# First weight block in halves, the second feed-forward's turn between products, and key-2 one-hots in pairs

## The chip, the cores and the metric

The kernel is one program on one NeuronCore of a Trainium2 chip. The metric is the device time of one execution in microseconds; the number that stands for a kernel is the median of its runs. All times below are microseconds from the start of the profiled execution's span unless they are marked otherwise.

## What is computed

Two blocks over 256 tokens of width 1024, all in float32:

```
h = x
f = swiglu(rmsnorm(h), ffn1_w_gu, ffn1_w_down)        # 1024 -> 2 x 2816 -> 1024
h = h + 0.5 * rmsnorm(f)
m = hybrid_mixer(rmsnorm(h))                          # attention and state space
h = h + rmsnorm(m)
c = memory_cross_attention(rmsnorm(h), rmsnorm(mem))
h = h + rmsnorm(c)
f = swiglu(rmsnorm(h), ffn2_w_gu, ffn2_w_down)        # the second feed-forward
h = h + 0.5 * rmsnorm(f)
# second block
x = x + mix @ w_out                                   # short convolution and HGRN2
x = x + peer_ffn(rmsnorm(x), wq, keys, u, v)          # product keys, 128 x 128 experts
return rmsnorm(x)
```

In `peer_ffn` each token picks 16 x 8 pairs (key 1, key 2) with gates. The expert weight of a token is gelu(h u) times its gate, and the result is the sum over all 16,384 experts of weight times v. The kernel computes all experts densely and multiplies by a gate matrix (128 keys 1 by 128 keys 2) for each token.

## The kernel before, in words

**Weights.** All large matrices are one stream of 532 blocks of 128 x 1024 f32 (512 KB). SP loads them into a ring of four slots (lines 368 to 384). Each product in float32 is made of three products in the fast f32r form, so each block is split first: ScalarE copies it to `w_high` (L503, helper `split`), VectorE subtracts to get `w_low` (L1049, the same helper on VectorE). `product` (L1848 to L1850) then makes three matmuls: high x high, high x low, low x high. Semaphores count: `w_high`, `w_split` (low part done; SP waits for it before it loads the slot again) and `w_used` (PE done with a block; ScalarE waits for it before it splits into the slot again).

**Activations.** Rows are tokens in two tiles of 128. Before a feed-forward the tile is transposed on PE, eight 128 x 128 transposes into PSUM (`turn_tile`, L1869). ScalarE copies each one with its gain to `xT_high` (`highs`, L540), VectorE makes `xT_low` (`lows`, L1088). PE waits for the low parts it needs (`turned`).

**Order.** Each engine has its own program, an order written out by hand, and waits on semaphores only; what stands behind a waiting instruction waits too. The order around the change is:

- Start. SP issues: left half of tile 0's rows, the small column table `cols` (gains), ring block 0, right half of tile 0's rows, block 1, tile 1's rows, blocks 2 and 3, and more. PE: `turn_tile(0, 0)` (all eight transposes, the last four wait for the right half), then `ffn_up` with `panel_by_tile`: for tile 0 the blocks 0 to 3 (two k tiles each, six matmuls of 512 columns a block), with `turn_tile(0, 1)` after block 0; then the same four blocks for tile 1. ScalarE: high copies of k tiles 0 to 3, split of block 0, high copies 4 to 7, splits 1 to 3, high copies of tile 1, two squares of the rows, then the splits of panel 1 (lines 609 to 624). VectorE the same with the low parts (lines 1163 to 1175).
- Second feed-forward. The output product of the cross attention ends with `rows_tail`: the last four blocks for tile 0, then for tile 1 (24 matmuls). VectorE adds tile 0's result to `h` (`post_add`, L1135, L1141, L1143), splits blocks 0 and 1 of the new panel, makes tile 0's low parts, splits block 2, adds tile 1's result, splits block 3, makes tile 1's low parts (lines 1435 to 1444). ScalarE: split 0 to 2, high copies of tile 0, square of tile 1's result, split 3, high copies of tile 1, two squares of `h`, then the splits of panel 1 (lines 815 to 825). PE: `turn_tile(6, 0)` after the tail, the products of blocks 0 to 2 for tile 0, `turn_tile(6, 1)`, block 3, then tile 1.
- Gated steps. From u block 66 on, PE alternates one u block (24 matmuls of 256 columns) with `gates`: for a group of four tokens eight f16 matmuls of 128 columns (L2459, L2460) that place the gates of one token at (key 2, key 1). The stationary operand is `one_at_key2` (OB), a one-hot of key 2 for each token; the moving one is the gate at key 1, in a high (OAH) and a low f16 part (OAL). VectorE makes the key-1 one-hot (`hot1`, L1730), the key-2 one-hot (`hot2`, L1738), the low gates (L1747), multiplies gates into the weights (L1756, L1767) and splits one weight block (L1049) a step. ScalarE makes gelu (L957), a weight copy and four gate copies (L967). The key-1 one-hots and OAL lie with two tokens innermost; the key-2 one-hots lie token by token. After the last u block PE waits for the last groups' operands and begins the v blocks (`v_half`); VectorE's last `hot2` there stands before the first low part of the expert weights (L1803).

The longest single names: `h_done` counts VectorE's result updates, `xt_ps` groups of four transposes, `xt_high` and `xt_low` single k tiles.

Of the kernel before, what the change touches and what calls it, by code (L numbers as in the profile page):

```python
# [16 lines left out]
P = 128  # L17
# [58 lines left out]
TAIL = 4  # L76
EPS_COL = 60
# [29 lines left out]
def build(nc, stream, w_dt, cols, small_row, rows, x, mem, keys, out):  # L107
# [127 lines left out]
    OB = sb("one_at_key2", [P, 2, GROUP, P], 68.5, F16)  # L235
# [47 lines left out]

    def hidden_psum(p):

        o = 1024 + (p - 9) * 512 if p >= FFN_PANELS - 2 else 2048 + p % 2 * 512
        return PS[:, o:o + 512]
# [21 lines left out]
    loaded = [sem(f"loaded{i}") for i in range(SLOTS)]  # L310
    w_high, w_split, w_used = sem("w_high_done"), sem("w_split_done"), sem("w_used")
# [7 lines left out]
    eps_ok, rms_ok, xn_ok, factor_ok = sem("eps_ok"), sem("rms_ok"), sem("xn_ok"), sem("row_factor_ok")  # L319
    xt_ps, xt_high, xt_low = sem("xT_psum"), sem("xT_high_done"), sem("xT_low_done")  # L320
# [46 lines left out]
    def _(sp):  # L367
        sp.dma_start(H[:, 0, 0:512], x[0:P, 0:512]).then_inc(x_in, 16)
        sp.dma_start(COLS[:], cols).then_inc(const_in, 16)
        sp.dma_start(RING[:, 0, :], stream[0]).then_inc(loaded[0], 16)  # L370
# [122 lines left out]
    def _(act):  # L493
# [41 lines left out]
        def highs(k, gain, tt, high=XTH, kts=range(KT)):  # L535

            for kt in kts:
                if kt % 4 == 0:
                    act.wait_ge(xt_ps, 4 * k + 2 * tt + kt // 4 + 1)
                act.activation(high[:, kt, tt * P:(tt + 1) * P], xt_psum(k, tt)[:, kt, :], ACT.Copy,  # L540
# [67 lines left out]

        act.preload_act_table_set("sqrt_and_others")
# [3 lines left out]
        split(0, 1)  # L613
# [428 lines left out]
    def _(dve):  # L1042
# [39 lines left out]
        def lows(k, gain, tt, high=XTH, low=XTL, kts=range(KT)):  # L1082

            t = slice(tt * P, (tt + 1) * P)
            for kt in kts:
                if kt % 4 == 0:
                    dve.wait_ge(xt_high, 16 * k + 8 * tt + kt + 4)
                dve.scalar_tensor_tensor(low[:, kt, t], xt_psum(k, tt)[:, kt, :],  # L1088
# [48 lines left out]
        def post_add(k, tt, factor, acc=ACC):  # L1137
# [4 lines left out]
                                           ROWG[:], ALU.mult, ALU.mult))  # L1142
            dve.scalar_tensor_tensor(H[:, tt, :], TMP[:, tt, :], factor, H[:, tt, :],  # L1143
# [22 lines left out]
        split(0, 1)  # L1166
# [271 lines left out]
        split(b + 4, 2)  # L1438
        lows(6, "ffn2", 0)
# [293 lines left out]
        def hot2(g, dyn=None):  # L1733

            if dyn is not None or g >= 2:
                dve.wait_ge(g_ps, at(g - 1, dyn))
            t = bass.ds(at(GROUP * g, dyn, GROUP), GROUP)
            dve.tensor_tensor(OB[:, g % 2, :, :], IOTA[:].unsqueeze(1).to_broadcast([P, GROUP, P]),  # L1738
                              KEY_T[:, 1, t].unsqueeze(2).to_broadcast([P, GROUP, P]),
                              ALU.is_equal).then_inc(key2_ok, 1)  # L1740
# [104 lines left out]
    def _(pe):  # L1845
# [6 lines left out]
        def turn_tile(k, tt, kts=range(KT)):  # L1852
# [3 lines left out]
            elif k == 6:  # L1856
                pe.wait_ge(h_done, 5 + tt)
# [8 lines left out]
            for kt in kts:  # L1866
                if k == 0 and tt == 0 and kt == 4:
                    pe.wait_ge(x_right_in, 16)
                last = pe.transpose(xt_psum(k, tt)[:, kt, :], rows[:, tt, kt * P:(kt + 1) * P], IDENT[:])  # L1869
                if kt % 4 == 3:  # L1870
# [711 lines left out]
```

## Time and profile before

| | |
|---|---|
| median of 3 runs | 1685.05 us (1684.35 to 1688.13) |
| the profiled execution, its own time | 1690.22 us |
| its span | 1688.2 us |
| PE busy | 1659.6 us, 98% |
| PE weight loads busy | 1477.2 us, 88% |
| VectorE busy | 1183.8 us, 70% |
| ScalarE busy | 935.7 us, 55% |
| GpSimd busy | 49.5 us, 3% |
| DMA | 286.78 MB, 170 GB/s over the span |

Busy times of PE overlap, since matmuls are pipelined and their ends are modelled. The distance from one start to the next tells more than the duration of one. A timeline row gives the start, the duration (of a group of equal instructions, all of it), engine, line, operation, output <- inputs, and in brackets how long the engine had been idle and what released it. In rows of groups the last numbers are busy us, mean ns of one, and idle us before them.

### The profile page before, as it was taken

What the parts mean: (1) busy time and instruction counts of PE and PEld (TensorE: products, weight loads), DVE (VectorE), ACT (ScalarE), POOL (GpSimd) and SP (SyncE); (2) the same over time, 40 slices, a digit from 0 to 9 for tenths busy, and PEclk for the clock granted to TensorE, in tenths of its full rate; (3) what the DMA queues carried; (4) which work ended last, traced back from release to release, by engine and by line L of the source; (5) the groups of instructions that cost most, each with busy time, mean ns of one, the idle gap of its engine ahead of it and who ended that gap; (6) DMA issues with size and microseconds to landing.
All of it is one profiled execution on the core that took longest, in us unless ns stands there. A gap on an engine that the chain in (4) does not pass through costs nothing.

```text
span 1688.2 us, 30628 instructions
## 1 busy us (share of the span) xinstructions
PE 1659.6 (98%) x10348; PEld 1477.2 (88%) x10348; DVE 1183.8 (70%) x1920; ACT 935.7 (55%) x1566; POOL 49.5 (3%) x44
## 2 busy tenths in 40 slices
PE   8999999999999999989999999999999999999998
PEld 6888898898898788879989999999999888888887
DVE  5555686598565655466665799989999866666664
ACT  6445545476655644456364444467777655555554
POOL 0000003000000000010010000100000000000000
PEclk9999999999999999999999999999999999999999
DMA  7555463333453555545354445454444465555553
GB/s 271 188 182 185 172 203 112 113 103 135 150 200 114 199 187 185 188 145 185 118 175 163 168 166 201 162 172 152 161 149 159 150 200 192 193 193 192 194 191 125
DMA packets 79101, 286.78 MB, mean 170 GB/s; under 512 B 8896, under 2 KB 9152, under 8 KB 78912
## 3 DMA queue, kind: packets, MB, share of 16 engines
q1 hardware_dynamic: 78176, 282.27, 49.1%
q0 software_dynamic: 864, 3.67, 0.6%
q8 instruction: 41, 0.67, 0.2%
q14 instruction: 20, 0.16, 0.0%
HBM read 284.86 MB, written 1.05 MB: 169 GB/s over the span
## 4 chain that ended last, share of the span: by engine, by line
PE 93%; DVE 4%; ACT 2%; issue 1%; DMA 0%; POOL 0%; SPq 0%; ACTq 0%; DVEq 0%; POOLq 0%
PE ps L1848 29%; PE ps L1850 28%; PE ps L1849 28%; DVE w_low L1049 1%; PE ps L2459 1%; PE ps L2460 1%; PE ps L1869 1%; PE ps L1951 1%; ACT w_high L503 1%; PE ps L2424 0%; PE ps L2231 0%; PE ps L2093 0%; PE ps L2111 0%; PE ps L2250 0%; DVE tmp L1141 0%
## 5 line engine op out<-in xcount | busy, mean ns | idle before, releaser
L1049 DVE TENSOR_TENSOR w_low<-ring,w_high 128x1024 fp32r<-128x1024 f32 x532 | 653.2, 1232 | 314.3 <-ACT w_high L503 312.4
L503 ACT ACTIVATE w_high<-ring 128x1024 fp32r<-128x1024 f32 x532 | 558.7, 1055 | 297.2 <-PE ps L1850 285.7
L1848 PE MATMUL ps<-xT_high,w_high 128*128 128x256 f32 x1472 | 424.1, 288 | 0.0
L1849 PE MATMUL ps<-xT_high,w_low 128*128 128x256 f32 x1472 | 416.8, 283 | 0.0
L1850 PE MATMUL ps<-xT_low,w_high 128*128 128x256 f32 x1472 | 416.6, 283 | 0.0
L1848 PEld LDWEIGHTS ps<-xT_high,w_high 128*128 128x128 f32 x1472 | 282.4, 192 | 2.0 <-issue 1.6
L1849 PEld LDWEIGHTS ps<-xT_high,w_low 128*128 128x128 f32 x1472 | 282.6, 192 | 0.7 <-issue 0.5
L1850 PEld LDWEIGHTS ps<-xT_low,w_high 128*128 128x128 f32 x1472 | 282.5, 192 | 0.0
L1848 PE MATMUL ps<-w_high,expert_w_high 128*128 128x512 f32 x512 | 199.9, 391 | 0.2 <-DVE expert_w_low L1803 0.2
L1850 PE MATMUL ps<-w_low,expert_w_high 128*128 128x512 f32 x512 | 199.7, 390 | 0.0
L1849 PE MATMUL ps<-w_high,expert_w_low 128*128 128x512 f32 x512 | 199.7, 390 | 0.0
L1848 PE MATMUL ps<-w_high,xT_high 128*128 128x512 f32 x464 | 186.5, 402 | 5.2 <-DVE xT_low L1088 4.2
L1850 PE MATMUL ps<-w_low,xT_high 128*128 128x512 f32 x464 | 183.0, 394 | 0.0
L1849 PE MATMUL ps<-w_high,xT_low 128*128 128x512 f32 x464 | 182.8, 394 | 0.0
L1017 ACT ACTIVATE expert_w_high<-expert_w 128x256 fp32r x124 | 51.8, 418 | 164.9 <-PE ps L1850 164.9
L1848 PEld LDWEIGHTS ps<-w_high,expert_w_high 128*128 128x128 f32 x512 | 96.5, 188 | 20.4 <-issue 0.5
L1849 PEld LDWEIGHTS ps<-w_high,expert_w_low 128*128 128x128 f32 x512 | 96.4, 188 | 20.2
L1850 PEld LDWEIGHTS ps<-w_low,expert_w_high 128*128 128x128 f32 x512 | 96.4, 188 | 20.0
L1821 DVE TENSOR_TENSOR expert_w_low<-expert_w,expert_w_high 128x256 fp32r<-128x256 f32 x124 | 52.7, 425 | 82.2 <-ACT expert_w_high L1017 82.2
L1848 PEld LDWEIGHTS ps<-w_high,xT_high 128*128 128x128 f32 x464 | 88.6, 191 | 24.7 <-issue 4.6
L1850 PEld LDWEIGHTS ps<-w_low,xT_high 128*128 128x128 f32 x464 | 88.4, 190 | 19.2
L1849 PEld LDWEIGHTS ps<-w_high,xT_low 128*128 128x128 f32 x464 | 88.6, 191 | 17.4
(404 smaller groups left out, 2227.5 us busy)
## 6 DMA issues: line engine op xcount, KB each, us to landing
ring<-in_stream SPq DMA_DIRECT2D x532, 512.0 KB, 3.4
row_gain<-in_rows POOLq DMA_DIRECT2D x4, 512.0 KB, 4.5
mem_sb<-in_mem SPq DMA_DIRECT2D x1, 1024.0 KB, 9.8
keys_sb<-in_keys POOLq DMA_DIRECT2D x1, 1024.0 KB, 5.2
h<-in_x SPq DMA_DIRECT2D x2, 256.0 KB, 3.9
h<-in_x SPq DMA_DIRECT2D x1, 512.0 KB, 6.9
last_gain<-in_rows POOLq DMA_DIRECT2D x1, 512.0 KB, 4.3
out<-result SPq DMA_DIRECT2D x1, 512.0 KB, 2.6
```

The source lines that it names most:

```text
L503: act.activation(WH[:, n % SLOTS, :], RING[:, n % SLOTS, :], ACT.Copy).then_inc(w_high, 1)
L1017: act.activation(WTH[:, v % 4, :], slot, ACT.Copy).then_inc(wt_high, 1)
L1049: dve.tensor_tensor(WL[:, n % SLOTS, :], RING[:, n % SLOTS, :], WH[:, n % SLOTS, :].bitcast(F32), ALU.subtract).then_inc(w_split, 1)
L1821: dve.tensor_tensor(WTL[:, v % 4, :], slot, WTH[:, v % 4, :].bitcast(F32), ALU.subtract).then_inc(wt_low, 1)
L1848: pe.matmul(out, high, w_hi, start=start, stop=False, skip_group_check=True)
L1849: pe.matmul(out, low, w_hi, start=False, stop=False, skip_group_check=True)
L1850: return pe.matmul(out, high, w_lo, start=False, stop=stop, skip_group_check=True)
L1869: last = pe.transpose(xt_psum(k, tt)[:, kt, :], rows[:, tt, kt * P:(kt + 1) * P], IDENT[:])
L1951: last = pe.transpose(hidden_psum(p)[:, o:o + P], HN[:, parity, tt, ft * P:(ft + 1) * P], IDENT[:])
L2459: pe.matmul(PS[:, o:o + P], OB[:, g % 2, j, :], OAH[:, g % 2, j, :], start=True, stop=False)
L2460: last = pe.matmul(PS[:, o:o + P], OB[:, g % 2, j, :], OAL[:, g % 2, j // 2, :, j % 2], start=False, stop=True)
```

## The change

What it does, part by part:

- **Start.** The load of `cols` is issued by ScalarE ahead of its table load. Block 0 is loaded in two halves of 512 columns, both ahead of the right half of tile 0's rows; ScalarE and VectorE split each half by itself. Tile 0's k tiles 0 to 3 are transposed into pairs of their own PSUM banks and copied pair by pair. Tile 0's k tiles 4 to 7 are transposed after block 0's products, tile 1's after block 1's.
- **Second feed-forward.** The result update of that stage is made in two halves with a semaphore each. `turn_tile(6, 0)` is moved ahead of the last block of the output product's tail, in two halves, into pairs of banks. VectorE splits one block, makes four low parts, splits one block, makes the other four. Tile 1's transposes are made four after block 2 and four after block 3.
- **Gated steps.** `one_at_key2` gets the layout of the key-1 one-hots, [pair, key, 2 tokens], and is compared against the f16 iota; PE reads it at a step of two values.

```diff
+HALVED = (2,)
...
-    OB = sb("one_at_key2", [P, 2, GROUP, P], 68.5, F16)
+    OB = sb("one_at_key2", [P, 2, GROUP // 2, P, 2], 68.5, F16)
...
+    def by_pairs(k, tt):
+        return k in (0, 6) and tt == 0
+    def xt_tile(k, tt, kt):
+        if by_pairs(k, tt):
+            o = 1024 + kt // 2 * 512 + kt % 2 * P
+            return PS[:, o:o + P]
+        return xt_psum(k, tt)[:, kt, :]
...
         sp.dma_start(H[:, 0, 0:512], x[0:P, 0:512]).then_inc(x_in, 16)
-        sp.dma_start(COLS[:], cols).then_inc(const_in, 16)
-        sp.dma_start(RING[:, 0, :], stream[0]).then_inc(loaded[0], 16)
+        sp.dma_start(RING[:, 0, 0:512], stream[0][:, 0:512]).then_inc(first_in, 16)
+        sp.dma_start(RING[:, 0, 512:1024], stream[0][:, 512:1024]).then_inc(loaded[0], 16)
         sp.dma_start(H[:, 0, 512:1024], x[0:P, 512:1024]).then_inc(x_right_in, 16)
...
             for kt in kts:
-                if kt % 4 == 0:
+                if by_pairs(k, tt) and kt < 4:
+                    if kt % 2 == 0:
+                        act.wait_ge(xt_pair, k // 3 + kt // 2 + 1)
+                elif kt % 4 == 0:
                     act.wait_ge(xt_ps, 4 * k + 2 * tt + kt // 4 + 1)
...
+        act.dma_start(COLS[:], cols).then_inc(const_in, 16)
         act.preload_act_table_set("sqrt_and_others")
         act.wait_ge(eps_ok, 1)
         act.wait_ge(const_in, 16)
         highs(0, "ffn1", 0, kts=range(0, 4))
-        split(0, 1)
+        act.wait_ge(first_in, 16)
+        act.activation(WH[:, 0, 0:512], RING[:, 0, 0:512], ACT.Copy).then_inc(first_high, 1)
+        act.wait_ge(loaded[0], 16)
+        act.activation(WH[:, 0, 512:1024], RING[:, 0, 512:1024], ACT.Copy).then_inc(w_high, 1)
         highs(0, "ffn1", 0, kts=range(4, 8))
         split(1, 3)
...
             for kt in kts:
-                if kt % 4 == 0:
+                if by_pairs(k, tt):
+                    if kt % 2 == 0:
+                        dve.wait_ge(xt_high, 16 * k + 8 * tt + kt + 2)
+                elif kt % 4 == 0:
                     dve.wait_ge(xt_high, 16 * k + 8 * tt + kt + 4)
...
+            if k in HALVED:
+                for half, done in enumerate((h_left, h_done)):
+                    w = slice(half * 512, half * 512 + 512)
+                    dve.scalar_tensor_tensor(H[:, tt, w], TMP[:, tt, w], factor, H[:, tt, w],
+                                             ALU.mult, ALU.add).then_inc(done, 1)
+                return
...
         lows(0, "ffn1", 0, kts=range(0, 4))
-        split(0, 1)
+        for half, high, low in ((0, first_high, first_low), (1, w_high, w_split)):
+            w = slice(half * 512, half * 512 + 512)
+            dve.wait_ge(high, 1)
+            dve.tensor_tensor(WL[:, 0, w], RING[:, 0, w], WH[:, 0, w].bitcast(F32), ALU.subtract).then_inc(low, 1)
...
         post_add(2, 0, 1.0)
-        split(b + 4, 2)
-        lows(6, "ffn2", 0)
+        split(b + 4, 1)
+        lows(6, "ffn2", 0, kts=range(0, 4))
+        split(b + 5, 1)
+        lows(6, "ffn2", 0, kts=range(4, 8))
         split(b + 6, 1)
...
-            t = bass.ds(at(GROUP * g, dyn, GROUP), GROUP)
-            dve.tensor_tensor(OB[:, g % 2, :, :], IOTA[:].unsqueeze(1).to_broadcast([P, GROUP, P]),
-                              KEY_T[:, 1, t].unsqueeze(2).to_broadcast([P, GROUP, P]),
-                              ALU.is_equal).then_inc(key2_ok, 1)
+            dve.tensor_tensor(OB[:, g % 2, :, :, :], IOTA16[:].unsqueeze(1).to_broadcast([P, GROUP // 2, P, 2]),
+                              pairs(KEY_T[:, 1, :], g, dyn), ALU.is_equal).then_inc(key2_ok, 1)
...
             elif k == 6:
-                pe.wait_ge(h_done, 5 + tt)
+                if 0 in kts:
+                    pe.wait_ge(h_left, tt + 1)
+                if 4 in kts:
+                    pe.wait_ge(h_done, 5 + tt)
...
                     for kt in (2 * n, 2 * n + 1):
+                        if tt == 0 and b + n == 0:
+                            pe.wait_ge((first_low, w_split)[kt], 1)
...
                     if tt:
                         last.then_inc(w_used, 1)
+                    elif norm == 0 and n == 0:
+                        turn_tile(0, 0, range(4, 8))
+                    elif norm == 6 and n == turn_after:
+                        turn_tile(norm, 1, range(0, 4))
+                    elif norm == 6 and n == turn_after + 1:
+                        turn_tile(norm, 1, range(4, 8))
                     elif n == turn_after:
                         turn_tile(norm, 1)
...
             last.then_inc(acc0_done, 1)
             for kt in range(kts - TAIL, kts):
+                if turn is not None and kt == kts - 1:
+                    turn_tile(turn, 0, range(0, 4))
+                    turn_tile(turn, 0, range(4, 8))
                 row_block(stage, kt, 1, high, low, acc, kts).then_inc(w_used, 1)
...
-        turn_tile(0, 0)
-        ffn_up("ffn1_up", 0, 0, 0)
+        turn_tile(0, 0, range(0, 4))
+        ffn_up("ffn1_up", 0, 0, 1)
...
-        rows_tail("xa_o", 8)
-        turn_tile(6, 0)
+        rows_tail("xa_o", 8, turn=6)
...
-                pe.matmul(PS[:, o:o + P], OB[:, g % 2, j, :], OAH[:, g % 2, j, :], start=True, stop=False)
-                last = pe.matmul(PS[:, o:o + P], OB[:, g % 2, j, :], OAL[:, g % 2, j // 2, :, j % 2],
+                pe.matmul(PS[:, o:o + P], OB[:, g % 2, j // 2, :, j % 2], OAH[:, g % 2, j, :], start=True, stop=False)
+                last = pe.matmul(PS[:, o:o + P], OB[:, g % 2, j // 2, :, j % 2], OAL[:, g % 2, j // 2, :, j % 2],
                                  start=False, stop=True)
```

## Rows read from the trace of the kernel before

**Rows 1.** The page, part 1: busy us, share, instructions.
```profile
PE 1659.6 (98%) x10348; PEld 1477.2 (88%) x10348; DVE 1183.8 (70%) x1920; ACT 935.7 (55%) x1566; POOL 49.5 (3%) x44
```
**Rows 2.** Waits of PE: waiter <- releaser, us in total, times, longest.
```profile
PE ps L1848 <- DVE xT_low L1088: 4.2, 2, 2.6
```
**Rows 3.** The chain that ended last, at the start: start us, us, what.
```profile
1.74 4.98 DMA ring<-in_stream
```
**Rows 4.** Timeline of PE at the start.
```profile
3.59 1.09 PE L1869 MATMUL ps<-ident,h 128*128 128x128 f32 x4 [3.59 <-DMA h<-in_x]
...
9.11 0.80 PE L1848 MATMUL ps<-w_high,xT_high 128*128 128x512 f32 x1 [0.52 <-DVE w_low L1049]
...
11.84 1.91 PE L1869 MATMUL ps<-ident,h 128*128 128x128 f32 x8
13.40 0.78 PE L1848 MATMUL ps<-w_high,xT_high 128*128 128x512 f32 x1
...
14.74 0.40 PE L1848 MATMUL ps<-w_high,xT_high 128*128 128x512 f32 x1
...
18.15 0.39 PE L1848 MATMUL ps<-w_high,xT_high 128*128 128x512 f32 x1
```
**Rows 5.** Timeline of ScalarE at the start.
```profile
4.80 1.14 ACT L540 ACTIVATE xT_high<-ps,cols 128x128 fp32r<-128x128 f32 x4 [2.71 <-PE ps L1869]
...
8.62 1.15 ACT L540 ACTIVATE xT_high<-ps,cols 128x128 fp32r<-128x128 f32 x4 [0.82 <-PE ps L1869]
9.64 1.07 ACT L503 ACTIVATE w_high<-ring 128x1024 fp32r<-128x1024 f32 x1
```
**Rows 6.** Timeline of VectorE at the start.
```profile
10.85 1.21 DVE L1049 TENSOR_TENSOR w_low<-ring,w_high 128x1024 fp32r<-128x1024 f32 x1
```
**Rows 7.** Groups of ScalarE, shapes apart: busy us, mean ns | idle.
```profile
L659 ACT ACTIVATE xn<-ssd_out 128x512 f32<-128x512 f32 x4 | 2.5, 629 | 0.1
```
**Rows 8.** Groups of VectorE, shapes apart.
```profile
L1738 DVE TENSOR_TENSOR one_at_key<-iota,keysT 128x512 f16<-128x512 f32 x64 | 43.4, 679 | 0.0
...
L1730 DVE TENSOR_TENSOR one_at_key<-iota,keysT 128x512 f16<-128x512 f16 x64 | 26.6, 416 | 0.9 <-ACT gate_low L991 0.9
```
**Rows 9.** Timeline of VectorE at the second feed-forward.
```profile
544.48 2.35 DVE L1049 TENSOR_TENSOR w_low<-ring,w_high 128x1024 fp32r<-128x1024 f32 x2
...
553.20 1.22 DVE L1049 TENSOR_TENSOR w_low<-ring,w_high 128x1024 fp32r<-128x1024 f32 x1
...
559.92 2.36 DVE L1049 TENSOR_TENSOR w_low<-ring,w_high 128x1024 fp32r<-128x1024 f32 x2 [0.79 <-ACT w_high L503]
```
**Rows 10.** Timeline of ScalarE at the second feed-forward.
```profile
554.02 2.18 ACT L540 ACTIVATE xT_high<-ps,cols 128x128 fp32r<-128x128 f32 x8 [3.41 <-PE ps L1869]
...
558.84 3.92 ACT L503 ACTIVATE w_high<-ring 128x1024 fp32r<-128x1024 f32 x4
```
**Rows 11.** Timeline of PE at the second feed-forward.
```profile
554.46 0.50 PE L1848 MATMUL ps<-w_high,xT_high 128*128 128x512 f32 x1
...
561.44 0.39 PE L1848 MATMUL ps<-w_high,xT_high 128*128 128x512 f32 x1
```
**Rows 12.** Timeline of PE in one gated step.
```profile
1203.63 0.28 PE L1850 MATMUL ps<-xT_low,w_high 128*128 128x256 f32 x1
1203.75 0.23 PE L2459 MATMUL ps<-gate_high_at_key,one_at_key 128*128 128x128 f16 x1
...
1204.19 0.36 PE L1848 MATMUL ps<-xT_high,w_high 128*128 128x256 f32 x1
```
**Rows 13.** Busy time by stretch: us; PE, PEld, DVE, ACT, POOL; clock, DMA.
```profile
1180.00:1230.00 50.00, 50.00 (x475) 49.36 (x474) 49.82 (x90) 37.33 (x90) 0.00 (x0) 1.00 0.44 153
```
**Rows 14.** Timeline of PE after the last u block.
```profile
1331.80 0.23 PE L2459 MATMUL ps<-gate_high_at_key,one_at_key 128*128 128x128 f16 x1 [2.11 <-ACT gate_high_at_key L967]
...
1332.79 0.76 PE L1848 MATMUL ps<-w_high,expert_w_high 128*128 128x512 f32 x1 [0.24 <-DVE expert_w_low L1803]
```
**Rows 15.** Busy time by stretch, there; the clock is the third number from the end.
```profile
1335.00:1336.00 1.00, 1.00 (x5) 0.76 (x4) 0.83 (x3) 0.00 (x0) 0.00 (x0) 0.71 0.01 4
```

More of the change, by code:

```diff
@@ L310, in build @@
     loaded = [sem(f"loaded{i}") for i in range(SLOTS)]
+    first_in, first_high, first_low = sem("first_half_loaded"), sem("first_half_high"), sem("first_half_split")
     w_high, w_split, w_used = sem("w_high_done"), sem("w_split_done"), sem("w_used")
@@ L319, in build @@
     eps_ok, rms_ok, xn_ok, factor_ok = sem("eps_ok"), sem("rms_ok"), sem("xn_ok"), sem("row_factor_ok")
+    xt_pair, h_left = sem("xT_psum_first_pairs"), sem("h_left_done")
     xt_ps, xt_high, xt_low = sem("xT_psum"), sem("xT_high_done"), sem("xT_low_done")
@@ L537, in highs @@
             for kt in kts:
-                if kt % 4 == 0:
+                if by_pairs(k, tt) and kt < 4:
+                    if kt % 2 == 0:
+                        act.wait_ge(xt_pair, k // 3 + kt // 2 + 1)
+                elif kt % 4 == 0:
                     act.wait_ge(xt_ps, 4 * k + 2 * tt + kt // 4 + 1)
-                act.activation(high[:, kt, tt * P:(tt + 1) * P], xt_psum(k, tt)[:, kt, :], ACT.Copy,
+                act.activation(high[:, kt, tt * P:(tt + 1) * P], xt_tile(k, tt, kt), ACT.Copy,
                                scale=COLS[:, GAIN_COL[gain] + kt:GAIN_COL[gain] + kt + 1]).then_inc(xt_high, 1)
@@ L1085, in lows @@
             for kt in kts:
-                if kt % 4 == 0:
+                if by_pairs(k, tt):
+                    if kt % 2 == 0:
+                        dve.wait_ge(xt_high, 16 * k + 8 * tt + kt + 2)
+                elif kt % 4 == 0:
                     dve.wait_ge(xt_high, 16 * k + 8 * tt + kt + 4)
-                dve.scalar_tensor_tensor(low[:, kt, t], xt_psum(k, tt)[:, kt, :],
+                dve.scalar_tensor_tensor(low[:, kt, t], xt_tile(k, tt, kt),
                                          COLS[:, GAIN_COL[gain] + kt:GAIN_COL[gain] + kt + 1],
@@ L1868, in turn_tile @@
                     pe.wait_ge(x_right_in, 16)
-                last = pe.transpose(xt_psum(k, tt)[:, kt, :], rows[:, tt, kt * P:(kt + 1) * P], IDENT[:])
-                if kt % 4 == 3:
-                    last.then_inc(xt_ps, 1)
+                last = pe.transpose(xt_tile(k, tt, kt), rows[:, tt, kt * P:(kt + 1) * P], IDENT[:])
+                if by_pairs(k, tt) and kt in (1, 3):
+                    last.then_inc(xt_pair, 1)
+                elif kt % 4 == 3:
+                    last.then_inc(xt_ps, 2 if by_pairs(k, tt) else 1)
         def turned(k, tt, kts):
@@ L1921, in panel_by_tile @@
                     s = (b + n) % SLOTS
-                    if tt == 0:
+                    if tt == 0 and b + n:
                         pe.wait_ge(w_split, b + n + 1)
@@ L1988, in rows_product, with rows_tail @@
                 row_block(stage, kt, 1, high, low, acc, kts).then_inc(w_used, 1)
-        def rows_tail(stage, kts, high=HTH, low=HTL, acc=ACC, halves=None):
+        def rows_tail(stage, kts, high=HTH, low=HTL, acc=ACC, halves=None, turn=None):
             for kt in range(kts - TAIL, kts):
```

## The prediction

> **What bounds the kernel now.** I read the page first. TensorE is busy for 98% of the span [rows 1], and the chain that ended last runs almost wholly over PE, so what counts is where PE stands still. PE's waits by releaser come next: apart from the first input rows, the largest is 4.2 us for VectorE's low parts of the turned activations, in two places [rows 2]. The change touches three places, read in their timelines: the start, the entry to the second feed-forward at 544 to 562 us, and the gated steps at 1121 to 1337 us.
>
> At the start the chain is: the first weight block lands at 6.72 [rows 3], ScalarE copies it, VectorE subtracts, PE starts its first product at 9.11 [rows 4]. All eight transposes of tile 0 are done by then. The six products of block 0 are followed by the eight transposes of tile 1, and block 1 starts at 13.40, tile 1 at 18.15 [rows 4]. The spacing of products tells the clock: six take 11.84 - 9.11 = 2.73 us, 0.43 each, which for 512 columns is 1.2 GHz; from 14.74 they stand 0.227 apart ((18.15 - 14.74) / 15), which is 2.4 GHz (the recorded granted clock reads 1.0 throughout this stretch, so the spacing is the witness). So the lower level costs 0.47 us per us.
>
> **Part A, the start.** Moving the small column table to ScalarE's queue costs one issue there (about 0.4 us before its table load) and ScalarE has nothing to do until 4.80 [rows 5]: nothing. On SP's queue one issue leaves and one comes, so every later load is issued as before; the split block moves in shorter rows, and block 1's copy stands at 9.64 with later copies waiting for loads; I expect them under 0.5 us later, and they will be needed 2 us later (below): nothing.
>
> 1. Four transposes take 1.09 us from 3.59 [rows 4], about 0.21 apart, so the first pair ends at 4.25, not 4.68. The high copies start 0.12 later, at 4.37, and take 1.02 us to the next instruction (8.62 to 9.64) [rows 5]: the left half's copy starts at 5.39 if the half has landed. That load is shown nowhere: it lies between the first rows' landing (3.59) and the whole block's (6.72) [rows 3, 4]; as it is half the bytes, issued 0.47 earlier, I take 4.9, in time.
> 2. A copy of 512 columns takes 0.63 [rows 7], a subtraction of that width 0.68 [rows 8]: copy to 6.02, low parts of two pairs to about 6.2, subtraction to 6.9, first product at 6.95. That is 2.15 earlier than 9.11. The right half follows in time even if it lands at 6.72.
> 3. But tile 0's right transposes now stand **behind** the six products of block 0, and ScalarE's program has their high copies ahead of block 1's copy. So: products to 6.95 + 2.73 = 9.7; four transposes 1.1, to 10.8; high copies 1.02, block 1's copy from 11.8 to 12.9 (1.07 [rows 5]); its subtraction 1.21 [rows 6], to 14.15. Block 1 starts at 14.2: **0.8 later** than 13.40. And tile 1's eight transposes, done before 13.40 in the old order, still lie ahead: 0.87 at the full clock (half of the 1.56 from 11.84 to 13.40, with its start-up).
> 4. PE is idle from 10.8 to 14.2. Before, PE worked on from 9.11 and the clock rose 5.4 us later (the row at 14.74 is the first short one). Elsewhere, PE resumes at 1331.80 after 2.11 us of idleness, is recorded below full clock, and is back during 1335 to 1336 (0.71, so at about 1335.4), 3.6 us later [rows 14, 15]. I take 4.5 us between these. From 14.2, 18 products and 8 transposes need 18 x 0.227 + 0.87 = 4.95 us at full clock, plus 0.47 x 4.5 = 2.1: tile 1 starts at 21.25, **3.1 us later** than 18.15.
>
> Bounds of A: full clock at once gives 19.15, +1.0; a left half that lands only at 6.72 (+1.2) with the lag of 5.4 gives +4.7. Behind it ScalarE's squares end at about 23.0, and its first copy of panel 1, needed with its subtraction by 26.7, is ready by 25.3: hidden.
>
> **Part B, the second feed-forward.** The old order waits here for low parts before its first product, the shorter of the two waits (4.2 - 2.6 = 1.6 us [rows 2]). The new one transposes tile 0 ahead of the last block of the output product and so starts about 1.4 earlier, near 546.6. But VectorE then sets the pace. Its work from 544.48 to 553.20 [rows 9] is the same: three subtractions, eight low parts, one result update. Its one idle stretch, waiting for the high copies, shrinks only by what the split updates cost more, as ScalarE is busy with a weight copy until then. So block 3's subtraction still starts at 553.2 and block 3's products at 554.4, as before (554.46 [rows 11]): the early start turns into waits of 0.35, 0.85, 0.7 and 1.3 us.
>
> What is new comes behind. Four of tile 1's transposes moved from VectorE's shadow to after block 3: tile 1 starts at 554.4 + 1.5 + 0.45 = 556.4. Their high copies, until now made at 554.02 to 556.04 [rows 10], end at 556.7 + 1.0 = 557.7. Then come two squares, 2.80 us to the first copy of panel 1 (556.04 to 558.84 [rows 10]): 560.5 instead of 558.84. Its subtraction came out at 559.92 + 1.23 = 561.15 [rows 9] for a PE that began panel 1 at 561.44 [rows 11], which is 0.25 of slack. Now it comes out 1.66 later, at 562.8. PE would have wanted it at 561.85, so panel 1 starts at about 562.85: **+1.4 us**. Bounds: +0.4 (the transposes alone) and +2.9 (PE works 0.45 of the 2.5 us before 554.4, and should the clock fall there, block 3 and the transposes take 1.5 longer).
>
> **Part C, key-2 one-hots.** The operation goes from f32 compare to the packed form of the key-1 one-hots: 679 to 416 ns [rows 8], 0.26 us a step. In the loop VectorE shows 49.82 of 50 us busy but PE 50.00 [rows 13], with no wait, so it buys nothing there. Only at the end does it lie on the chain: PE waits 0.24 for the first low part of the weighted experts, right after such a one-hot [rows 14]: **-0.2 us**. TensorE now loads those one-hots at a step of two values. The rows show no such load; bounds are nothing and the rival below. I take nothing, since the moving operand of every second product is already read at that step and the eight products take 0.44 us [rows 12], evenly spaced.
>
> **The sum**: 3.1 + 1.4 - 0.2 = **+4.3 us**. The profiled execution took 1690.22 us (span 1688.2), 5.2 above the median of 1685.05; the difference carries over: 1689.4.
>
> **Rivals.**
> - Clock back early (0.18). PE works 3.8 us before its pause at the start, more than the 3.6 us of the other place. For: that figure. Against: the idle stretch after it is longer than the 2.11 us that cost the clock before. A is then +1.0, the sum +2.2: 1687.3.
> - More lost (0.15): late left half, slow clock at both places, about +6.5: 1691.6.
> - VectorE holds the gated loop (0.08), the one that ends on the other side, not slower. Place: 61 steps. PE's own work in a step is 24 products 0.12 apart and eight in 0.44 [rows 12], 3.32; a step takes about 3.37 (475 starts in 50 us at 32 a step [rows 13]). If these 0.05 to 0.07 are waits that the trace doesn't mark, a VectorE 0.26 faster gives them all back, -3 to -4.3; it decides if VectorE's step is the longer by any amount. With A and B it ends within 1.5 us of before: 1686. Against: PE shows no idle time and the first product after the one-hots is 0.08 longer wherever it stands.
> - Slow weight loads (0.08). If spaced f16 weights load as f32 ones do, whose products stand 0.12 apart [rows 12], eight take 0.96 instead of 0.44: 64 x 0.52 = +33, 1722. No row here decides between the two; by the first reading the sum would be that of this rival, by the second it stays.
> - The start pays off as drawn up, through an order that I misread (0.06): -2.2 and less, 1682.
>
> **Chances.** About 0.2% (3.4 us) is what a measurement of this kernel can tell from no change. My forecast has 0.45, mostly (0.36) beyond 3.4 us; with "more lost" and slow loads: slower 0.60. Same: the rest of the forecast, the early clock and the held loop: 0.33. Faster: 0.07. The range leaves out slow loads and the last rival: 1685.0 to 1694.0, A's and B's bounds included for the most part.
>
> **What would show it.** Start: first product near 7.0; a PE idle stretch of over 3 us before block 1, released by w_low after xT_high copies; block 1 near 14.2; products 0.43 apart until about 18.7; tile 1 near 21. Second feed-forward: first product near 546.6, then waits for w_low and h; block 3 unmoved against the start of the stage; panel 1 1.4 later with a wait for w_low behind ScalarE's squares. Gates: L1738's successor at about 416 ns, step length and product spacing unchanged, VectorE with 0.26 us of idle time a step. I am wrong if block 1 starts before 13.4, if the second feed-forward's first up panel ends earlier than before, or if the step changes.

## The result and the profile after

| | before | after |
|---|---|---|
| median of 11 runs each | 1687.41 us | 1692.12 us |
| lowest to highest | 1684.02 to 1691.1 | 1690.95 to 1693.0 |
| the profiled execution, its own time (span) | 1690.22 (1688.2) | 1693.0 (1691.0) |

The ratio is 1.0025, with a 95% interval of 1.0016 to 1.0034: slower by about 4.2 us (2.7 to 5.7 by the interval; the medians differ by 4.7), forecast +4.3. In this comparison the kernel before itself came out at 1687.41, 2.4 above the median of three runs that the forecast started from, so the absolute number is 2.7 above the forecast of 1689.4 and inside its range.

The page after: the engines' busy time, and, from the view of waits, four groups of PE's waits (us in total, times, longest).

```profile
PE 1659.6 (98%) x10348; PEld 1476.1 (87%) x10348; DVE 1170.5 (69%) x1923; ACT 934.3 (55%) x1567; POOL 49.4 (3%) x44
```

```profile
PE ps L1881 <- DVE w_low L1070: 6.6, 6, 3.4
PE ps L1905 <- DMA h<-in_x: 4.0, 1, 4.0
...
PE ps L1881 <- DVE xT_low L1112: 2.6, 1, 2.6
PE ps L1881 <- DVE w_low L1199: 2.3, 1, 2.3
```

Two more groups of that view, of the kernel before:

```profile
PE ps L1869 <- DMA h<-in_x: 6.4, 2, 3.6
...
PE ps L1848 <- DVE w_low L1049: 1.8, 4, 0.7
```

PE is busy as long as before; VectorE is busy 13 us less. PE waits 2.4 us less for input rows and 1.6 less for low parts of the activations (4.2 in [rows 2], 2.6 after), but for low parts of **weights** 6.6 + 2.3 = 8.9 us instead of 1.8. The balance is 3.1 more.

**The start.** The timeline of PE after, from the first transposes to tile 1 (21.19), and the granted clock (third number from the end) in two windows of it:

```profile
4.03 1.09 PE L1905 MATMUL ps<-ident,h 128*128 128x128 f32 x4 [4.03 <-DMA h<-in_x]
7.42 0.77 PE L1881 MATMUL ps<-w_high,xT_high 128*128 128x512 f32 x1 [2.30 <-DVE w_low L1199]
...
10.11 1.02 PE L1905 MATMUL ps<-ident,h 128*128 128x128 f32 x4
14.56 0.79 PE L1881 MATMUL ps<-w_high,xT_high 128*128 128x512 f32 x1 [3.43 <-DVE w_low L1070]
...
17.29 1.28 PE L1905 MATMUL ps<-ident,h 128*128 128x128 f32 x8
18.33 0.48 PE L1881 MATMUL ps<-w_high,xT_high 128*128 128x512 f32 x1
18.65 0.40 PE L1882 MATMUL ps<-w_high,xT_low 128*128 128x512 f32 x1
...
21.19 0.39 PE L1881 MATMUL ps<-w_high,xT_high 128*128 128x512 f32 x1
```

```profile
14.00:15.00 1.00, 0.43 (x1) 0.44 (x2) 1.00 (x2) 1.00 (x2) 0.00 (x0) 0.69 1.06 383
...
17.00:18.00 1.00, 1.00 (x7) 0.80 (x6) 0.00 (x0) 0.00 (x0) 0.00 (x0) 0.61 0.73 213
```

The first product starts 1.69 earlier than before, block 1 starts 1.16 later, tile 1 3.04 later (9.11, 13.40, 18.15 in [rows 4]). ScalarE and VectorE in the same stretch:

```profile
11.17 1.14 ACT L557 ACTIVATE xT_high<-ps,cols 128x128 fp32r<-128x128 f32 x4 [4.09 <-PE ps L1905]
12.18 2.96 ACT L517 ACTIVATE w_high<-ring 128x1024 fp32r<-128x1024 f32 x3
```

```profile
13.28 3.50 DVE L1070 TENSOR_TENSOR w_low<-ring,w_high 128x1024 fp32r<-128x1024 f32 x3 [0.33 <-ACT w_high L517]
```

ScalarE is idle for 4.09 us for want of the right transposes, with block 1's copy queued behind them. Only at 12.18 does that copy begin, and PE has its low part at 14.56. The granted clock falls at about 14.4, after PE has stood still for three microseconds, and is back at about 17.8, 3.2 us after block 1 began.

**The second feed-forward.** PE's rows with waits, and ScalarE's (block 3 begins at 557.39, the four transposes behind it at 558.89):

```profile
553.53 0.50 PE L1881 MATMUL ps<-w_high,xT_high 128*128 128x512 f32 x1 [0.49 <-DVE w_low L1070]
555.65 0.66 PE L1905 MATMUL ps<-ident,h 128*128 128x128 f32 x4 [0.46 <-DVE h L1170]
557.39 0.50 PE L1881 MATMUL ps<-w_high,xT_high 128*128 128x512 f32 x1 [1.08 <-DVE w_low L1070]
...
565.75 0.47 PE L1881 MATMUL ps<-w_high,xT_high 128*128 128x512 f32 x1 [0.80 <-DVE w_low L1070]
```

```profile
559.53 1.14 ACT L557 ACTIVATE xT_high<-ps,cols 128x128 fp32r<-128x128 f32 x4 [2.04 <-PE ps L1905]
...
563.31 3.89 ACT L517 ACTIVATE w_high<-ring 128x1024 fp32r<-128x1024 f32 x4
```

The stage comes 3.03 late (the x32 group at 520.03 instead of 517.00). With that taken off, panel 1 (565.75) starts 1.28 later than the 561.44 of [rows 11], after a wait of 0.80 behind ScalarE's squares. To compare stretches, I use the time from the x32 group ahead of the cross attention's output to the first group of turns of the feed-forward's hidden values. The chain that ended last has these rows before:

```profile
517.00 6.91 PE ps L2250 x32
...
572.49 0.44 PE ps L1951 x4
```

and these after, so the stretch grew from 55.49 to 56.85:

```profile
520.03 6.91 PE ps L2299 x32
...
576.88 0.44 PE ps L1997 x4
```

**The gated steps.** The groups of VectorE from 1140 to 1320 us, the key-2 one-hots, and the window that answers to [rows 13]:

```profile
L1772 DVE TENSOR_TENSOR one_at_key<-iota,keysT 128x512 f16<-128x512 f16 x53 | 21.9, 413 | 0.0
```

```profile
1180.00:1230.00 50.00, 50.00 (x471) 49.35 (x470) 46.78 (x89) 36.68 (x89) 0.00 (x0) 1.00 0.45 157
```

679 became 413 ns, and VectorE's busy time in 50 us fell from 49.82 to 46.78, while PE is as full as it was.

### The profile page after: what moved, and what is told of

Its sections match the earlier page's. It is cut to its first block, busy times and chain, and to the rows that moved or that the text cites. A ratio compares the mean times of both kernels' runs of the same rounds, so it can differ in the third digit from the quotient of the medians.

```text
span 1691.0 us, 30634 instructions
## 1 busy us (share of the span) xinstructions
PE 1659.6 (98%) x10348; PEld 1476.1 (87%) x10348; DVE 1170.5 (69%) x1923; ACT 934.3 (55%) x1567; POOL 49.4 (3%) x44
## 3 DMA queue, kind: packets, MB, share of 16 engines
q0 software_dynamic: 864, 3.67, 0.7%
## 4 chain that ended last, share of the span: by engine, by line
PE 93%; DVE 4%; ACT 2%; issue 1%; DMA 0%; POOL 0%; ACTq 0%; DVEq 0%; POOLq 0%
PE ps L1881 28%; PE ps L1882 28%; PE ps L1883 28%; DVE w_low L1070 1%; PE ps L2507 1%; PE ps L2508 1%; PE ps L1905 1%; ACT w_high L517 1%; PE ps L1997 1%; PE ps L2472 0%; PE ps L2280 0%; PE ps L2142 0%; PE ps L2160 0%; PE ps L2299 0%; DVE tmp L1165 0%
```

## The experiments

All kernels ran on one core, beside runs of the kernel before. What the texts on record call "the changed kernel" is the kernel after. Product, copy and turn lines shift by a few from kernel to kernel.

**1. Each part alone.** The start alone, then the second feed-forward alone, then the one-hots alone; the diff of the change is cut to that part.

> The start's part of the change alone. If the new order of the start costs what the changed kernel shows there (my theory): block 1's first product at 14.2 to 14.6, products 0.43 apart until about 18, tile 1 at 21.2 (18.15 before), every later stage up to the second feed-forward 3.0 us late, and the second feed-forward no further behind; ratio to before 1.0018. Rival, chance clock dips make the difference of the two kernels: ratio within 0.1% of 1.

Median 1693.39, ratio 1.0034 (1.0022 to 1.0046), above the 1.0018 that I expected and above the whole change. Block 1 at 14.76, tile 1 at 21.82: +3.67. The second feed-forward's stretch is 55.53, as before. The nine times lie in two groups, 1690.65 to 1691.87 with a mean granted clock of 0.995 or 0.996 (four runs) and 1693.39 to 1694.13 with 0.992 or 0.993 (five), and the median falls into the second. Why five of nine lie there isn't shown.

> The second feed-forward's part alone. My theory: block 3's products start where they did (554.4), tile 1 of panel 0 at 556.2, panel 1 at 562.8 instead of 561.4 with a PE wait of about 0.8 us for w_low behind ScalarE's two squares; +1.4 us from there on, ratio 1.0008. Rival, the early start of block 0 is kept: panel 1 at 560 to 561.

Median 1689.44, ratio 1.0008 (0.9997 to 1.0019). The stretch is 56.87: +1.38.

> The key-2 one-hots in pairs alone. My theory: L1738's operation at 413 ns, loads of these one-hots at 96 to 97 ns as before, gated step unchanged at 3.39 us, PE's wait before the first expert product 0.25 shorter: -0.2 us in all, ratio 0.9999. Rival, VectorE held the loop: step at 3.32 to 3.34, ratio 0.998.

Median 1686.78, ratio 0.9998 (0.9989 to 1.0008). One-hots 414 ns. The last gate's product to the first product of the experts fell from 0.56 (1332.23 to 1332.79 before) to 0.31, the forecast -0.25.

So by the traces each part does alone what it does in the sum. The ratios alone wouldn't show this: they add up to 1.0040 where the whole change has 1.0025, and those of the last two can't be told from 1.

**2. Block 1's parts ahead of the right rows' parts.** The kernel after with, on both ScalarE and VectorE:

```
+        split(1, 1)
         highs(0, "ffn1", 0, kts=range(4, 8))
-        split(1, 3)
+        split(2, 2)
```

> The changed kernel with one swap at the start: ScalarE's copy of block 1 and VectorE's subtraction stand ahead of the high and low parts of tile 0's right k tiles. My theory: block 1's copy starts when its load lands (about 9.0), its subtraction ends at 11.3, block 1's products at 11.4 instead of 14.56, the clock up near 12.8, tile 1 at 17.2 (21.19 in the changed kernel, 18.15 before): 4 us less than the changed kernel, ratio to before 1.0002. Rival, loads in shorter rows or the column table's other queue are the cost: block 1 no earlier than 13.

Median 1689.59, ratio 1.0003 (0.9992 to 1.0014). PE's timeline:

```profile
7.89 0.77 PE L1883 MATMUL ps<-w_high,xT_high 128*128 128x512 f32 x1 [2.30 <-DVE w_low L1200]
...
11.22 0.47 PE L1883 MATMUL ps<-w_high,xT_high 128*128 128x512 f32 x1
11.54 0.39 PE L1884 MATMUL ps<-w_high,xT_low 128*128 128x512 f32 x1
...
14.90 0.50 PE L1883 MATMUL ps<-w_high,xT_high 128*128 128x512 f32 x1 [1.18 <-DVE w_low L1071]
...
17.80 0.39 PE L1883 MATMUL ps<-w_high,xT_high 128*128 128x512 f32 x1
```

Block 1 follows with no wait, 3.3 us earlier, the products stand 0.23 apart from there on, and tile 1 starts 3.4 earlier. Tile 1 is 0.6 later than I expected, as block 2 now waits 1.18 behind the high copies. That the queue order behind the moved transposes makes the start's loss is shown by this: same halves, same moved transposes, same queue for the column table, no loss.

**3. The clock's share of it.** The kernel after with eight products behind the right transposes whose result is never read:

```
+                        for _ in range(8):
+                            pe.matmul(PS[:, 3072:3584], XTH[:, 0, 0:P], WH[:, 0, 0:512], start=True, stop=True)
```

> The changed kernel with eight products of 512 columns more, behind tile 0's right transposes at the start; their result is never read, they only keep TensorE busy while it otherwise waits for block 1. If the share of the start's loss that I put down to the clock is right (from 14.56 to 21.19 us the products and transposes take 6.6 us where full clock needs 4.95), block 1 starts at 14.5 to 14.9 as in the changed kernel, its products stand 0.23 us apart at once, and tile 1 starts at 19.4 to 20.0 instead of 21.2: ratio about 1.0016. If the clock has no part in it, tile 1 stays at 21.2 or later and the ratio at 1.0025.

Median 1689.89, ratio 1.0021 (1.0011 to 1.0031). PE:

```profile
11.05 2.08 PE L1974 MATMUL ps<-w_high,xT_high 128*128 128x512 f32 x8
14.73 0.50 PE L1881 MATMUL ps<-w_high,xT_high 128*128 128x512 f32 x1 [1.61 <-DVE w_low L1070]
15.07 0.39 PE L1882 MATMUL ps<-w_high,xT_low 128*128 128x512 f32 x1
...
19.86 0.39 PE L1881 MATMUL ps<-w_high,xT_high 128*128 128x512 f32 x1
```

Block 1 comes when it did (14.73 beside 14.56), since the eight products unblock nothing. But the products stand 0.23 apart at once, and tile 1 starts at 19.86 instead of 21.19. With block 1's 0.17 taken off, the clock lost in the pause is 1.5 of the 3.04, and the rest is the pause itself. The granted clock of the kernel after agrees: it lost 1.7 us between 14 and 18 us, and nothing is recorded there here. I forecast 2.1 for the clock. The median, 1.0021, can't be told from the 1.0025 of the kernel after; this rests on the traces.

**4. Tile 1 turned in one piece after block 2.** The kernel after with:

```
                     elif norm == 6 and n == turn_after:
-                        turn_tile(norm, 1, range(0, 4))
-                    elif norm == 6 and n == turn_after + 1:
-                        turn_tile(norm, 1, range(4, 8))
+                        turn_tile(norm, 1)
```

> The changed kernel with one thing undone in the second feed-forward: tile 1's eight transposes all stand after weight block 2, none after block 3. My theory of the loss there (four transposes behind block 3, so ScalarE's high copies of tile 1, its two squares and its copy of panel 1 all start later, and TensorE waits for panel 1's low part) expects the stretch from the first x32 group of the cross attention (520.03 in the changed kernel) to the group of turns behind the feed-forward (576.88) to shrink from 56.85 to 55.5 to 55.9 us, as it was before (55.49), and no wait for w_low at panel 1. The rival, that the loss comes from turning tile 0 early (split updates, a pause of TensorE that costs it its clock), expects 56.5 to 57. Ratio to the kernel before: 1.0017 by the theory, 1.0025 by the rival.

The timeline of PE and of ScalarE:

```profile
556.67 1.06 PE L1905 MATMUL ps<-ident,h 128*128 128x128 f32 x8 [1.15 <-DVE h L1170]
557.72 0.51 PE L1881 MATMUL ps<-w_high,xT_high 128*128 128x512 f32 x1
```

```profile
562.15 1.99 ACT L517 ACTIVATE w_high<-ring 128x1024 fp32r<-128x1024 f32 x2
```

The stage begins at 520.36 here (0.33 later than in the kernel after) and yet panel 1's copies begin at 562.15 instead of 563.31. PE shows no wait behind the turn, and the stretch is 55.45: the loss is gone, though tile 0 is still turned early and `h` still updated in halves. The theory holds in the trace. The time doesn't show the gain: median 1691.7, ratio 1.0033 (1.0023 to 1.0043), where I had expected 1.0017. Its profile lost 1.7 us more to the clock elsewhere than that of the kernel after (experiment 7), and of its other nine runs three have a mean granted clock as low (0.992 or 0.993). The other six have 0.996 and average 1691.3 us; the six runs of the kernel after at 0.996 average 1691.8. So at an equal clock 0.5 of the 1.4 us shows in the times, and where the rest stays is open.

**5. A kernel with the gains and without the losses.** The kernel before with the split first block and the start's moved transposes, experiment 2's order and the paired one-hots.

> The kernel before with the split first block, block 1's copy and subtraction ahead of those of tile 0's right rows, and the key-2 one-hots two tokens innermost; the second feed-forward as before. If the two losses are where I put them (block 1 queued behind the right rows; tile 1's transposes behind block 3), this keeps the gains and has neither loss: block 1 at 11.2 to 11.8, tile 1 at 17.2 to 17.9 (18.15 before), the feed-forward's stretch 55.5, the last gate step 0.25 shorter: 0.5 to 1.2 us faster than before, ratio 0.9993 to 0.9997. If a shared cause that I have not found is at work, it stays above 1.0005.

Block 1 at 11.17, tile 1 at 17.63, the stretch 55.55. Median 1688.39, ratio 1.0008 (0.9999 to 1.0017): not faster, against my 0.9993 to 0.9997. I had compared its start with the 18.15 of one profile; the five profiles with the old start (experiment 7) have tile 1 at 17.74 on average, so its start gains 0.1, and part C (-0.25 at the end, +0.4 from the spaced loads of experiment 6) costs it that. The clock adds to that: its twelve runs have a mean granted clock of 0.9951, the 33 runs of before beside them 0.9958. That is 1.2 us, about what the ratio shows. Then the same with work for PE ahead of its first product:

```
+        for _ in range(5):
+            pe.matmul(PS[:, 3072:3200], IDENT[:], IDENT[:], start=True, stop=True)
         turn_tile(0, 0, range(0, 4))
+        for _ in range(5):
+            pe.matmul(PS[:, 3072:3200], IDENT[:], IDENT[:], start=True, stop=True)
```

> The previous kernel with five transposed identity products of 128 columns ahead of the first four transposes and five behind them; their result is never read, they only give TensorE work before its first product. If the clock at the start comes up by how long TensorE has been at work, the six first products stand 0.23 us apart rather than 0.43 in part or whole, and tile 1 starts 0.5 to 1.3 us earlier than in the previous kernel (if block 1's data is there; else block 1 waits for it and gains less than 0.5). If it comes up at a fixed lag after the first product only, nothing changes: tile 1 at 17.2 to 17.9.

PE's timeline:

```profile
1.60 2.50 PE L2056 MATMUL ps<-ident 128*128 128x128 f32 x10 [1.60 <-POOL ident L416]
...
7.98 0.59 PE L1881 MATMUL ps<-w_high,xT_high 128*128 128x512 f32 x1 [0.17 <-DVE w_low L1200]
8.41 0.40 PE L1882 MATMUL ps<-w_high,xT_low 128*128 128x512 f32 x1
...
11.53 0.50 PE L1881 MATMUL ps<-w_high,xT_high 128*128 128x512 f32 x1 [1.36 <-DVE w_low L1071]
```

The first products stand 0.23 apart instead of 0.43: the clock follows what PE did before them. Up to block 1 all of that is given back, as block 1 now isn't ready (a wait of 1.36): from the first product to block 1 it takes 3.55 us, and 3.62 without the early work. What stays is block 1's own products at the full clock and fewer later waits. Tile 1 starts at 16.95, 0.68 earlier, and the median is 1686.7, ratio 1.0 (0.9991 to 1.0009): level with before.

**6. The spaced weight load.** Comparing long stretches of steps showed something that single rows hide. Sixty gated steps in the kernel before and in the one with the pairs alone:

```profile
1125.86 0.23 PE L2459 MATMUL ps<-gate_high_at_key,one_at_key 128*128 128x128 f16 x1 [0.95 <-ACT gate_high_at_key L967]
...
1329.06 0.23 PE L2459 MATMUL ps<-gate_high_at_key,one_at_key 128*128 128x128 f16 x1
```

```profile
1119.55 0.23 PE L2457 MATMUL ps<-gate_high_at_key,one_at_key 128*128 128x128 f16 x1 [0.94 <-ACT gate_high_at_key L967]
...
1323.14 0.23 PE L2457 MATMUL ps<-gate_high_at_key,one_at_key 128*128 128x128 f16 x1
```

203.20 / 60 = 3.387 us, and 203.59 / 60 = 3.393. All kernels with pairs have the second, all without the first. One kernel keeps VectorE's slow f32 compare but writes to the spaced layout, which PE reads as in the change:

```
-            dve.tensor_tensor(OB[:, g % 2, :, :], IOTA[:].unsqueeze(1).to_broadcast([P, GROUP, P]),
+            dve.tensor_tensor(OB[:, g % 2, :, :, :].rearrange("p a k b -> p a b k"), IOTA[:].unsqueeze(1).unsqueeze(1).to_broadcast([P, GROUP // 2, 2, P]),
```

> The kernel before with its key-2 one-hots written at a step of two values (so TensorE loads them spaced, as in the changed kernel), but from the f32 table and by the f32 compare, so that VectorE's operation stays slow. A gated step takes 3.387 us in every kernel without the pairs and 3.393 in every one with them. If the spaced load is the cause, the step here is 3.393; if VectorE's shorter operation is (its traffic or its timing beside TensorE), it stays at 3.387. Either way the last gate step to the first expert product is 0.55 us as before, or more.

One run, 1688.69 us. The groups of VectorE and PE's weight loads from 1140 to 1320, and the window of 50 us:

```profile
L1738 DVE TENSOR_TENSOR one_at_key<-iota,keysT 128x512 f16<-128x512 f32 x54 | 41.3, 766 | 0.0
```

```profile
L2459 PEld LDWEIGHTS ps<-gate_high_at_key,one_at_key 128*128 128x128 f16 x212 | 19.4, 97 | 2.3
```

```profile
1180.00:1230.00 50.00, 50.00 (x475) 49.36 (x474) 50.00 (x89) 36.72 (x89) 0.00 (x0) 1.00 0.46 157
```

Sixty steps run from 1123.60 to 1327.20: 3.393. So the spaced operand costs 6.6 ns a step, some 0.4 us in all, whatever VectorE does. And VectorE, with its one-hots at 766 ns and busy for 50.00 of 50, still doesn't lengthen the step: it doesn't hold the loop.

**7. The two kernels once more, and the account.** The times scatter by 7 us within a kernel, and experiments 4 and 5 came out above their traces.

> The kernel before, profiled once more. The three kernels so far that keep its start show tile 1 at 18.15, 18.52 and 16.98 us, and the ten profiles so far lose their clock in pieces of 1.7 us. If the start's scatter is that of the first rows' landing and of the moment at which the clock rises, tile 1 starts between 16.9 and 18.6 again, the second feed-forward's stretch is 55.5 us and a gated step 3.387 us to within 0.002. With the lost clock taken off, the span is 1678.0 plus the difference of tile 1 to 18.15, within 0.3. If the scatter lies elsewhere, that sum misses by more.

> The changed kernel, profiled once more. By the accounts (start, second feed-forward, gated steps, lost clock in pieces of 1.7 us) tile 1 starts between 21.0 and 21.9 us, the second feed-forward's stretch is 56.85, a gated step 3.393, and with the lost clock taken off the span is 1682.5 plus the difference of tile 1 to 21.19, within 0.3. If the changed kernel's loss were chance of its first profile, one of these misses.

A window of the first profile of before (the last three numbers are PE's clock, the DMA share and GB/s), and PE's rows around it:

```profile
250.00:251.00 1.00, 1.00 (x7) 1.00 (x7) 1.00 (x4) 0.89 (x2) 0.00 (x0) 0.57 0.05 16
```

```profile
247.56 0.17 PE L1848 MATMUL ps<-w_dt_high,xT_high 128*128 128x16 f32 x1
...
250.41 0.36 PE L1849 MATMUL ps<-w_dt_high,xT_low 128*128 128x16 f32 x1
...
255.31 0.77 PE L1848 MATMUL ps<-w_high,xT_high 128*128 128x512 f32 x1
```

PE shows as busy without a gap, and its granted clock falls to 0.50 for some ten us. But what keeps it busy from 247.56 to 255.31 are 48 products of only 16 columns (the state space's step sizes, `w_dt`), 0.11 us apart at first and 0.21 at half clock; it falls 2.6 us into them. All 13 profiles have the 48 products and the fall there. In seven the fall comes 2.3 to 2.8 us after the first of them and the clock stays down for about 10.2 us; in four it comes after 3.3 to 4.4 us and lasts 6.8; in the two others (before again, pairs alone) after 5.1 to 5.2 us, at their end, and lasts 3.4.

I summed (1 - granted clock) over every window of 2 us between 50 and 1680 us. In all 13 profiles the loss comes in pieces of 1.7 us: one to three around 250 us; one or two near 742, where PE is idle for 1.5 and 2.6 us around eight transposes; one near 802 in three kernels, at the end of 32 products of 32 rows; one near 1331 in all but one, after 2.1 us of idleness. (The start, before 50 us, is left out, as tile 1's row accounts for it.) With these taken off, the spans fit a sum of 1678.0 (the first profile of before: 1688.2 - 10.2) + (tile 1 - 18.15) + (stretch - 55.49) + 0.4 for spaced loads - 0.25 for the short one-hot at the end:

| kernel | tile 1 | stretch | clock lost | span less that | by the sum |
|---|---|---|---|---|---|
| before, again | 17.57 | 55.50 | 5.1 | 1677.6 | 1677.4 |
| start alone | 21.82 | 55.53 | 6.8 | 1681.8 | 1681.7 |
| second feed-forward alone | 18.52 | 56.87 | 8.5 | 1679.6 | 1679.7 |
| pairs alone | 16.98 | 55.54 | 5.1 | 1677.2 | 1677.0 |
| after | 21.19 | 56.85 | 8.5 | 1682.5 | 1682.6 |
| after, again | 21.53 | 56.85 | 8.5 | 1682.9 | 1682.9 |
| block 1 first | 17.80 | 56.88 | 8.5 | 1679.2 | 1679.2 |
| filled | 19.86 | 56.89 | 6.8 | 1681.0 | 1681.2 |
| tile 1 in one piece | 21.53 | 55.45 | 10.2 | 1681.7 | 1681.5 |
| gains without losses | 17.63 | 55.55 | 8.5 | 1677.8 | 1677.7 |
| the same, with early work | 16.95 | 55.56 | 8.5 | 1677.0 | 1677.0 |
| spaced only | 17.48 | 55.51 | 8.5 | 1678.2 | 1677.7 |

Eleven of twelve close within 0.2 us; the last, whose one-hots are slower than before's, misses by 0.5. So nothing else above a few tenths of a us is needed to account for the traces. The number of pieces is what scatters: three to six among the kernels' single profiles, three against six for the same kernel before. A ratio between medians carries this, up to a piece, on top of the mechanisms. The mean granted clocks of all runs say how much: 0.9953 and 0.9958 for the kernel before in two sets of 32 and 33 runs, 0.9951 and 0.9953 for the two kernels of experiment 5, where 0.001 is 1.7 us. Whether a change shifts the number of pieces, or the runs only drew them, they don't settle.

## Why the prediction was right

**What bounds it.** PE's stretch of waits decided, and busy shares did not: VectorE's 13 us fewer bought a quarter of a microsecond, at the end of the loop.

**Part A, predicted +3.1, measured +3.04** against the first profile of before. Tile 1 at 21.19 (I said 21.25), block 1 at 14.56 (14.2). That it came within 0.1 is luck, since the steps had errors that cancel. The first rows landed at 4.03, not 3.59, so the first product came at 7.42 instead of 6.95, the pause began later, and block 1 came 0.36 later than I had it. The clock came back sooner, by its record at about 17.8, 3.2 us after block 1 began, where I had used 4.5: from block 1 to tile 1 it took 6.63 us, not 7.05. The other place that I used ([rows 15]) I had misread by 0.2: a clock of 0.71 in 1335 to 1336 puts its return at 1335.6, 3.8 us after PE resumed. Against all profiles the loss is larger: five with the old start have tile 1 at 16.98 to 18.52 (mean 17.74), four with the new one at 21.19 to 21.82 (mean 21.52), +3.8. That is inside the bounds of +1.0 to +4.7; that the old start itself moves by 1.5 from run to run I had not priced.

**Part B, predicted +1.4, measured +1.36** (and 1.38 alone). The chain was as drawn: block 3 unmoved, four transposes behind it, high copies, two squares, the first copy of panel 1, its subtraction, PE waiting. Tile 0's early start was worth nothing, since VectorE set the pace. Panel 1 itself was 1.28 later, where I said 1.4.

**Part C, predicted -0.2, measured +0.15**: -0.25 at the end as forecast, and +0.4 from the spaced loads. The step that failed is "I take nothing" for the load: eight products in 0.44 us still take 0.43 to 0.44, but the step is 6.6 ns longer. Averaged over 52 steps, the positions of its 32 products show that it comes behind them, among the products of 256 columns; why, no run here tells. The figure is far from the rival's, that eight loads would take 0.96; its 0.12 was the distance of products of 256 columns, and nothing showed that their loads set it.

**The sum**: 3.04 + 1.36 + 0.15 = +4.55 against the profiles' own 1682.5 - 1678.0 = +4.5 with the lost clock off, forecast +4.3. The two profiled spans differ by only 2.8, because before drew one piece of lost clock more. Against the mean of the old starts in place of 18.15 the parts add up to +5.3, which is inside the interval of the measured times too (+2.7 to +5.7); so that 4.2 came so near to 4.3 is in part luck too.

**The rivals.** "Clock back early" fell: products stood 0.43 apart from 14.56 on. With PE kept busy for the first 2.1 us of the pause, part A would have been 19.86 - 18.15 = +1.7. "More lost": not met. "VectorE holds the loop" fell twice, by the pairs alone (413 ns, no shorter step) and by 766 ns with the same step. So none of the 0.05 to 0.07 us that might have been hidden waits in a step was VectorE's. "Slow weight loads" fell: 97 ns a load, beside 96 and 97 before, and by the sentence of the Trainium skill (TensorE: Matmul & The Clock Gate, "Weight-path perf modes") that columns may be packed or strided, the trace nearly agrees, up to those 6.6 ns. "The start pays off" fell by 3 to 4 us.

**The base** was the largest error: the median of three runs was 1685.05, and 1687.41, 1687.49 and 1685.94 came from 11, 32 and 33 runs.

## What to carry to other kernels

To start PE sooner, look at what its next wait hangs on. Here the transposes were moved behind the first products, and in ScalarE's hand-written order the copy of block 1 stood behind their copies; a first product 1.7 us earlier became a pause of 3.4 us, and of the 3.0 us that this cost, 1.5 were clock. Before an operation is moved on one engine, follow each consumer's queue and move what does not need it ahead of it.

When single changes of 1 or 2 us are at stake, compare stretches between the same rows in both traces and take the lost clock off; medians of a dozen runs don't resolve them here. A row of windows that says "busy 1.00" doesn't say that the clock holds: read the granted clock beside it, and look at what the products in it are.

## What I had not expected of the hardware

- PE's granted clock can fall to 0.50 with no idle time in the profile before it. In all 13 profiles it does so within 2.3 to 5.2 us of the first of 48 back-to-back products of 16 columns, 0.11 us apart (250.2 us above), and costs 1.7 to 5.1 us there; the earlier it falls among them, the longer it stays down. No run here changes these 48 products, so what another order of them would save isn't shown. Runs of the kernel before spread from 1683.89 to 1691.23; its two profiles differ by 5.5 in span, 5.1 of that in lost clock.
- The start of one kernel varies by over a microsecond: three old starts have the right rows' transposes at 7.76 to 7.90, released by their load, and block 1's first products were at half clock in one (13.70 to 14.27, 0.57 apart) and at full clock in another (13.38 to 13.69). The Trainium skill (TensorE: Matmul & The Clock Gate, Part 1) says that the count of slow products at the start varies from run to run of one kernel; these traces agree.
- Five f32 identity products of 128 columns (ten records, 2.50 us) ahead of the first transposes and five behind them were enough for the first weight products to run 0.23 apart from the second on.
- A spaced stationary operand in f16 costs 1 ns or less on its own load record, and 6.6 ns a step of 32 products behind it.
